# Modulation sums in four pieces between pieces of projections, and layer norms behind the experts by half rows

## What is computed

```python
def first_block(...):                     # one layer
    c_act = jax.nn.silu(c)
    mod = (c_act @ ada_w[i] + ada_b[i])   # 1024 -> 6*1024: six slices
    h = rmsnorm(x, g) * (1.0 + sc1) + sh1
    x = x + g1 * rmsnorm(windowed_gqa_sink(h, ...), ...)
    h = rmsnorm(x, ...) * (1.0 + sc2) + sh2
    x = x + g2 * rmsnorm(swiglu(h, ffn_w_in, ffn_w_out), ...)

def second_block(...):                    # two layers, with modulations of their own
    for i in range(2):
        sh1, sc1, g1, sh2, sc2, g2 = jnp.split(silu_c @ ada_w[i] + ada_b[i], 6, axis=-1)
        yx = mixer_ab(...) if i == 0 else mixer_pool(...)   # differential attention + gate; pooling
        xs = layer_norm(alpha * xs + g1 * yx, ln_g[i, 0], ln_b[i, 0])
        hx = modulate(xs, sh2, sc2)
        fx = peer(hx, peer_wq[i], peer_keys[i], peer_u[i], peer_v[i])   # 128 experts a token, gathered
        xs = layer_norm(alpha * xs + g2 * fx, ln_g[i, 1], ln_b[i, 1])
    return xs

def layer_norm(h, g, b):
    mu = jnp.mean(h, axis=-1, keepdims=True)
    var = jnp.mean(jnp.square(h - mu), axis=-1, keepdims=True)
    return (h - mu) * lax.rsqrt(var + LN_EPS) * g + b
```

## Time and profile before

| | us |
|---|---|
| median of 3 runs | 2122.01 (2121.99 to 2124.06) |
| the profiled execution's own time | 2130.78 |
| its span, first to last instruction | 2128.9 |
| feed-forward input, 22 parts | about 222 to 336 |
| feed-forward output, 11 parts | about 336 to 405 |
| product stage | about 429 to 690 |
| expert stage 0, expert stage 1 | about 725 to 1381, 1480 to 2118 |
| norm and output of token tile 1 | 2117.8 to 2128.9 |

### The profile page before, as it was taken

How to read it: one execution, slowest core, us unless ns; L and a number is a source line. 1 busy time by engine, 2 the same in 40 slices (tenths; PEclk the granted TensorE clock), 3 DMA queues, 4 the chain that set the end, 5 groups by cost and what they waited for, 6 DMA issues and landing times.

```text
span 2128.9 us, 22402 instructions
## 1 busy us (share of the span) xinstructions
PE 1796.7 (84%) x7293; PEld 1085.8 (51%) x7293; DVE 1458.7 (69%) x3023; ACT 911.5 (43%) x2383; POOL 617.7 (29%) x573
## 2 busy tenths in 40 slices
PE   4888999899998899997777787988998877877776
PEld 3757998788887544443222222455654422322222
DVE  6676857677866767766676677527677667677675
ACT  2446433434464344444344444424444444444442
POOL 1160000000000434444334334213444444443441
PEclk9888989899999899999999999999999999999999
DMA  9753758555664899999999999966999999999995
GB/s 368 278 198 119 263 192 298 199 203 213 218 218 144 320 421 421 421 421 420 419 421 422 421 421 421 371 239 273 409 415 421 421 421 421 422 421 421 421 422 242
DMA packets 114693, 723.80 MB, mean 340 GB/s; under 512 B 11504, under 2 KB 13344, under 8 KB 34064
## 3 DMA queue, kind: packets, MB, share of 16 engines
q0 software_dynamic: 74864, 540.30, 61.3%
q1 hardware_dynamic: 39712, 182.07, 23.4%
HBM read 721.24 MB, written 1.08 MB: 339 GB/s over the span
## 4 chain that ended last, share of the span: by engine, by line
DMA 36%; PE 31%; DVE 16%; ACT 7%; issue 5%; POOL 3%; another core or an unknown queue 0%; SPq 0%; DVEq 0%; ACTq 0%; POOLq 0%
DMA X<-in_k_uv,EI 20%; DMA Z<-in_k_uv,EI 12%; PE PS L2183 11%; PE PS L1875 3%; PE PS L1876 3%; PE PS L1877 3%; DVE junk L1862 3%; PE PS L2159 3%; DVE WL L1505 3%; DVE ACC L1489 3%; DMA W<-in_k_uv,EI 2%; POOL X L1047 2%; PE PS L1968 2%; DMA W<-in_ada_w 2%; ACT WH L1056 1%
## 5 line engine op out<-in xcount | busy, mean ns | idle before, releaser
L2183 PE MATMUL PS<-X,dg 128*128 128x512 f32 x1380 | 663.5, 613 | 132.1 <-ACT dg L1056 131.0
L1862 DVE CUSTOM_DVE_ANT_0 junk<-H,X 128x1024 f32<-128x1024 f32 x345 | 421.9, 1223 | 244.5 <-DMA X<-in_k_uv,EI 232.2
L1047 POOL DMA_INDIRECT X<-in_k_uv,EI x345 | 370.1, 1073 | 509.4 <-PE PS L2183 307.8
L2183 PEld LDWEIGHTS PS<-X,dg 128*128 128x128 f32 x1380 | 248.8, 193 | 507.3 <-ACT dg L1056 295.4
L1056 ACT ACTIVATE CF<-DOT 128x1 f32<-128x1 f32 x512 | 103.6, 202 | 666.2 <-DVE DOT L1862 662.6
L2183 PE MATMUL PS<-Z,dg 128*128 128x512 f32 x480 | 237.2, 621 | 65.1 <-ACT dg L1056 64.9
L1056 ACT ACTIVATE dg<-CP,CG 128x128 f32<-128x128 f32 x512 | 205.5, 401 | 17.6 <-PE PS L2183 1.0
L1862 DVE CUSTOM_DVE_ANT_0 junk<-H,Z 128x1024 f32<-128x1024 f32 x120 | 146.8, 1223 | 94.4 <-DMA Z<-in_k_uv,EI 90.9
L2183 PEld LDWEIGHTS PS<-Z,dg 128*128 128x128 f32 x480 | 84.2, 191 | 198.3 <-ACT dg L1056 132.8
L1875 PE MATMUL PS<-XH,WH 128*128 128x256 f32 x592 | 177.0, 299 | 3.6 <-DVE WL L1505 2.1
L1876 PE MATMUL PS<-XL,WH 128*128 128x256 f32 x592 | 172.7, 292 | 0.0
(11 more groups left out here) (314 smaller groups left out, 2599.5 us busy)
## 6 DMA issues: line engine op xcount, KB each, us to landing
W<-in_ada_w SPq DMA_DIRECT2D x56, 1024.0 KB, 5.3
Y<-in_ada_w SPq DMA_DIRECT2D x16, 1024.0 KB, 5.9
W<-in_k_win SPq DMA_DIRECT2D x16, 1024.0 KB, 5.0
W<-in_k_ffi SPq DMA_DIRECT2D x13, 1024.0 KB, 6.0
Y<-in_k_ffi SPq DMA_DIRECT2D x9, 1024.0 KB, 4.9
W<-in_ffn_w_out SPq DMA_DIRECT2D x8, 1024.0 KB, 5.6
W<-in_peer_wq SPq DMA_DIRECT2D x8, 1024.0 KB, 13.0
W<-in_ab_w_out SPq DMA_DIRECT2D x6, 1024.0 KB, 5.2
```

What stands on the lines that cost most here:

```text
L1047: e.indirect_dma_start(out=WS[k][:, :], out_offset=None, in_=I[f"k_uv{ly}"][:, :], in_offset=bass.IndirectOffsetOnAxis(ap=EI[t][:, j:j + 1 ...
L1862: e.tensor_tensor_reduce(junk, H[:, t, :], d[:, 0:D], 1.0, 0.0, ALU.mult, ALU.add, DOT[:, j:j + 1]).then_inc(v_dot, 1)
L2183: p = e.matmul(PS[:, 2 * t + q, :], dgb[n % 4][:, :], d[:, D + q * 512:D + (q + 1) * 512], start=(j == 0), stop=(j == 127))
```

## The change

**Sums in pieces.** A new `gemm_mod(n, s)` places a quarter of part n, then a quarter of sum s (four of its 16 columns), four times over, and `mod` behind. It is used for i = 16 with s = 3, for i = 17 with s = 4, and for i = 7 of the output with s = 5. In the product stage a sum that is due goes out in four pieces, one in each following gap (`sums()`), from the first call of `step` after its eighth slab on; `mod` follows the fourth. `step` may now be called in 14 gaps k = 0 instead of 12. In TensorE's program `modp` takes the bank with its first piece and signals with its last.

**Norms by halves.** `brn` and `frn` multiply, add and take statistics of columns 0 to 511 first, and of columns 512 to 1023 then. The first half waits for a new semaphore `p_lo`, which the first 512-column matmul of a tile's last expert gives. In `frn 1` a new `finish` merges the normalisation with scale and shift: for each half (x - mean) * R5, and then times the reciprocal root plus R1; the first of these passes stands ahead of the wait for ScalarE's root. Step `x, 7` is gone. The output of tile 1 leaves in two DMAs of 256 KB.

```diff
+    def gemm_mod(n, s, *banks):
+
+        for q in range(4):
+            P("gq", n, q, *banks)
+            P("modp", s, 3, q)
+        P("mod", s, 3)
...
-        if i == 16:
-            mod(3, 3)
-            mod(4, 3)
-        gemm(n, bank(low))
+        if i in (16, 17):
+            gemm_mod(n, i - 13, bank(low))
+        else:
+            gemm(n, bank(low))
...
         if i == 7:
-            mod(5, 3)
-        gemm(n)
+            gemm_mod(n, 5)
+        else:
+            gemm(n)
...
-    due = []
+    due, ripe = [], []
 
     def step(b):
 
-        if len(due) > 1:
-            mod(due[0], b)
-            due.clear()
-        elif due:
-            due.append(None)
+        if due:
+            ripe.append(b)
             return
         m = next(steps, None)
         if m is not None:
             ada(m)
             if m in mods:
-                due.append(mods[m])
+                due.extend((mods[m], part) for part in range(4))
+
+    def sums():
+
+        if due and ripe:
+            s, part = due.pop(0)
+            P("modp", s, ripe[0], part)
+            if part == 3:
+                P("mod", s, ripe[0])
+                ripe.clear()
...
-    places = (1, 2, 3, 4, 5, 6, 7, 8, 9, 10, 11, 13)
+    places = range(14)
...
     P("frn", 1)
-    P("x", 7)
     P("out", 1)
...
+            def sum_halves(name, t, y, row, done):
+
+                for half in range(2):
+                    z = slice(512 * half, 512 * half + 512)
+                    w.wait_ge(p_dg if half else p_lo, done if half else done // 128)
+                    q = e.tensor_tensor(H[:, t, z], y[:, z], row[:, z], ALU.mult)
...
+                    e.scalar_tensor_tensor(out=XS[:, t, z], in0=XS[:, t, z], scalar=ALPHA, in1=H[:, t, z],
+                                           op0=ALU.mult, op1=ALU.add).then_inc(v_own, 1)
+                    w.wait_ge(v_own, own.up())
+                    e.bn_stats(bs[:, t, half, :], XS[:, t, z]).then_inc(v_own, 1)
...
+                for half, c in enumerate(halves):
+                    e.scalar_tensor_tensor(out=XS[:, t, c], in0=XS[:, t, c], scalar=mv[:, t, 0:1], in1=R[5][:, c],
+                                           op0=ALU.subtract, op1=ALU.mult).then_inc(v_own, 1)
+                    if half == 0:
+                        w.wait_ge(a_rt, place)
+                        e.reciprocal(z, z).then_inc(v_rs, 1)
+                        w.wait_ge(v_rs, place)
+                    w.wait_ge(v_own, own.up())
+                    e.scalar_tensor_tensor(out=XS[:, t, c], in0=XS[:, t, c], scalar=z, in1=R[1][:, c],
+                                           op0=ALU.mult, op1=ALU.add).then_inc(v_x, 1)
...
+                    lo, hi = (4 * a[2], 4 * a[2] + 4) if len(a) > 2 else (0, 16)
...
-                    for j in range(16):
+                    for j in range(lo, hi):
...
+                        if j == 127 and q == 0:
+                            p.then_inc(p_lo, 1)
```

More of the change, by code:

```diff
@@ L284, in make_plan @@
             step(5)
+        sums()
         next(g)
@@ L981, in _ @@
                     t = a[0]
-                    w.wait_ge(v_x, nth("x", 6 + t))
                     ov = out.rearrange("b (t p) d -> p (b t) d", p=128)
-                    e.dma_start(ov[:, t, :], XS[:, t, :]).then_inc(d_out, 16)
-            w.wait_ge(d_out, 32)
+                    w.wait_ge(v_x, nth("x", 6) + t)
+                    if t:
+                        e.dma_start(ov[:, t, 0:512], XS[:, t, 0:512]).then_inc(d_out, 16)
+                        w.wait_ge(v_x, nth("x", 6) + 2)
+                        e.dma_start(ov[:, t, 512:1024], XS[:, t, 512:1024]).then_inc(d_out, 16)
+                    else:
+                        e.dma_start(ov[:, t, :], XS[:, t, :]).then_inc(d_out, 16)
+            w.wait_ge(d_out, 48)
         @block.gpsimd
@@ L1386, in normalize @@
                 z = mv[:, t, 1:2]
+                e.tensor_scalar(z, z, LN_EPS, None, ALU.add).then_inc(v_ms, 1)
+                return z
+            def normalize(name, t):
+                z = spread_of(t)
                 place = nth.rs[name]
-                e.tensor_scalar(z, z, LN_EPS, None, ALU.add).then_inc(v_ms, 1)
                 w.wait_ge(a_rt, place)
@@ L1392, in normalize, with finish @@
                 e.tensor_scalar(XS[:, t, :], XS[:, t, :], mv[:, t, 0:1], z, ALU.subtract, ALU.mult).then_inc(v_rn, 1)
+            def finish(name, t):
+                z = spread_of(t)
+                place = nth.rs[name]
+                halves = [slice(512 * half, 512 * half + 512) for half in range(2)]
+                w.wait_ge(d_r5, 64)
+                w.wait_ge(d_r1, 64)
+                for half, c in enumerate(halves):
[5 more added lines that the diff above has]
+                        w.wait_ge(v_rs, place)
+                    w.wait_ge(v_own, own.up())
+                    e.scalar_tensor_tensor(out=XS[:, t, c], in0=XS[:, t, c], scalar=z, in1=R[1][:, c],
+                                           op0=ALU.mult, op1=ALU.add).then_inc(v_x, 1)
             def affine(dst, src, grow, brow):
@@ L1965, in _ @@
                     w.wait_ge(v_ada, vada(8 * MOD_SLICE[s] + 7))
-                    take(b)
-                    for j in range(16):
+                    if lo == 0:
+                        take(b)
+                    for j in range(lo, hi):
                         p = e.matmul(PS[:, b, j:j + 1], src[:, j * 128:(j + 1) * 128], ones[:, 0:1],
                                      start=True, stop=True)
-                    p.then_inc(p_mod, 1)
-                    free[b] = [(v_mod, s + 1)]
+                    if hi == 16:
+                        p.then_inc(p_mod, 1)
+                        free[b] = [(v_mod, s + 1)]
                 elif kind == "xp":
```

29 lines of the change are left out of this document (20 added, 9 removed).

## The result

The changed kernel took 2111.62 us (median of five runs, 2110.99 to 2114.28); the kernel before, in five runs, 2124.06 (2121.99 to 2126.79). The ratio is 0.9937 with a 95% interval of 0.9921 to 0.9952, so it is faster by 0.5 to 0.8%. The forecast was 2107.0 with a range of 2102 to 2117: a gain of 15.0 us against 12.4 between the medians, or 13.4 by the ratio.

What follows compares the result with a forecast made beforehand. Ahead of the experts, TensorE paces the first block's feed-forward and parts of the product stage, VectorE with ScalarE the others. 7.1 + 1.35 + 7.5 - 2.45 + 1.45 = 15.0 us off the median 2122.0 gives 2107.0, range 2102 to 2117.

Steps and rivals of the forecast that it cites:

- A: Feed-forward input: sums 3 and 4 in quarters between quarters of parts 26 and 27, 7.1 us gained.
- D: Norms by halves and smaller last DMA: nothing between the layers, 1.45 us gained at the kernel's end.
- B: Part 39: sum 5 in quarters, so eight 512-column passes avoid the lower clock, 1.35 us gained.
- C: Product stage: sums 6, 7 and 8 in quarters, 7.5 us gained together, less 2.45 us for moved slabs.
- Sum 6: Product stage, where TensorE sets the pace: 1.25 us gained from the clock, with its changes between matmuls.
- Sum 7: Product stage, where ScalarE waited for the K part: 2.7 us from the clock plus 0.87, 3.5 gained.
- Sum 8: Product stage: 2.5 us from the clock plus a little of its own last passes, 2.8 gained.
- slab 65: Product stage, VectorE: moved from an idle stretch to ahead of unit 12's maximum, 1.1 us late (0 to 2.35).
- Slab 71: Between the last OB scaling and the turn of XT, on VectorE: 1.35 us lost (0 to 2.35).
- The first: Product stage: VectorE and ScalarE swallow half or more of the sums' gain; total gain 10 us, 2112; chance 0.20.
- a fall whatever the order: All cut sums: pieces bring the clock down as long as whole sums; gain nil, 2122 to 2120; chance 0.10.
- a clock low over all of a part: Parts with pieces: interleaving holds the clock at 0.50 throughout; about 25 us slower, 2147; chance 0.08.

Runs made afterwards that it cites:

- e4_no_c: Changed kernel with the product stage as before: sums 6 to 8 whole, slabs in their old places; 2115.93 us, ratio 0.9956 to the kernel before.
- e6_tail_only: Kernel before with only the new norms and the output in two halves; ratio 0.9986 to the kernel before.
- e1_banks: Kernel before with sum 4 in bank 4 instead of bank 3, so it no longer waits for sum 3's reader; 2125.42 us.
- e2_whole: Changed kernel with sums 3 and 4 whole, one ahead of part 26 and one ahead of part 27; 2114.56 us.
- e5_early: Changed kernel with three slabs of the product stage in other places, none ahead of unit 12's maximum; 2112.08 us, ratio 0.9931 to the kernel before.
- e3_halves: Changed kernel with sums 3 to 8 in two pieces of eight columns instead of four pieces of four; 2120.09 us.

## Why the prediction was right, and where its terms were off

The time, the sign and the range held: 2111.6 in 2102 to 2117, 12.4 to 13.4 us where 15.0 were forecast. Of the four parts A and D came, each 0.4 above its forecast; B is not shown; of C, 5.0 with its slabs, 2.1 to 4.4 came, against the traces with whole sums of e4_no_c and e6_tail_only. Together that is 7.5 + 0 + 2.1 to 4.4 + 1.8, or 11.4 to 13.7 us, and fits the time.

**A, forecast 7.1: 7.5**, in every trace of the code with pieces. The mechanism was right; only the price of changing between matmuls was nearly nothing. The forecast's own sum had slipped there: six changes at 0.08 are 0.48 a part, and it booked 0.24 (part 26 would take 9.74, not 9.5, and A would be 6.6 to 6.7). Both alternatives that would have undone it are out: the clock falls without the idle wait too (e1_banks), and behind a single whole sum (e2_whole).

**B, forecast 1.35: not shown.** The first pair of traces differs by 1.55 in this stage, which looks like a hit, but the second trace of the old code lacks the difference. The step that failed was to take the eight slow passes of the earlier trace rows for a property of the code. The stage took 73.59 with pieces and 73.59 with the whole sum in the second trace of that code. Two kernels with 72.0, one with a whole and one with a cut sum, lack another low stretch of the same stage (328 to 332 in the changed kernel). With a low stretch in one trace of three behind the whole sum, and in none of eight over the pieces, pieces may save half a microsecond there over many runs (an estimate, a third of 1.55); these runs can't tell.

**C, forecast 7.5 for the sums less 2.45 for the slabs: 2.1 to 5.8.** Against the first trace of before the stages 6 to 8 and the turn shrink by 3.5 in the first trace of the changed kernel and by 5.8 in the second; against e4_no_c by 2.1 and 4.3; against e6_tail_only (235.01) by 2.2 and 4.4. Sum 6, forecast 1.25, gave 1.6 or, against the other three traces with whole sums, 3.2. Sum 7, forecast 3.5, gave 1.8 to 4.8. Sum 8, forecast 2.8, reached unit 11's exponentials (2.7 us more lead) and was gone at unit 12. The term mis-sized is slab 65: taken at 1.1 out of 0 to 2.35, it lay there with its whole 2.3 between the weight split and the maximum, and the experiment without it gave back 1.6; the other 0.9 are lost at this place in e5_early too, and what they are stays open. Stage 8 as a whole is no better than before, and 1.5 worse than in e4_no_c. What the clock gave in it and what the new places of the slabs took can be told apart, because the whole sum 8 of e1_banks had no low stretch. The whole stage, in e1_banks (sum whole, slabs in their old places) and in the changed kernel:

```profile
547.26:630.31 83.05, 74.81 (x535) 65.02 (x534) 63.39 (x94) 50.95 (x100) 0.00 (x0) 0.98 0.61 214
540.36:626.21 85.85, 77.07 (x551) 67.42 (x551) 63.48 (x94) 51.15 (x99) 0.00 (x0) 0.98 0.58 209
```

At the same mean clock the changed kernel takes 2.8 us longer (2.7 in its second trace). The trace of before, with the product stage of e1_banks and 6.8 us at the lower clock at sum 8, takes 2.8 more as well; its other low stretch of this stage, at 629 to 637, hardly counts, since e4_no_c with 6.8 us and e6_tail_only with 3.4 us there both take 84.35. So the clock's share of sum 8 was forecast rightly (2.8), and the new order of the stage took all of it back, where 1.1 was booked.

**Slab 71, forecast 1.35 lost: the number was met and the reason was not.** The turn is 1.36 longer in the first trace, 0.8 in the second. But e5_early has the same 1.38 without the slab, and e3_halves has the slab without them. The time was that of passes at the lower clock behind TensorE's idle time of 2.2 us, an idle time that the trace of before and e3_halves have too, with the clock at 1.00 behind it. So this term cost nothing that the runs show. Had only the first trace been read, the wrong cause would have stood as shown.

**D, forecast 1.45: 1.8.** VectorE began 0.75 before the last matmul's end (0.86 forecast). The fused add took 0.69 with a fixed factor, where I had taken the 0.75 of an operation with a factor per row. From the first operation to the statistics it is 4.23 (forecast 4.34). From there to the last DMA 3.4 us, against 3.6 forecast (whose terms add up to 3.76) and 4.2 before. The last DMA took 2.5 until the end of the span against 3.1 with twice the bytes: 0.6, where I had taken 0.5. No run takes the halves, the merged passes and the two DMAs apart; this split is read from the timelines alone.

**The rivals.** The first, that VectorE and ScalarE swallow part of C, is what happened at sum 8, by a slab that the change itself had put there; the 10 us that it gave in all are 2.4 to 3.4 less than were measured, the forecast's 15.0 are 1.6 to 2.6 more. The runs lie between the two. That the measured 2111.6 falls on this rival's 2112 is an accident of the base (below). Pieces among small matmuls and transposes did keep the clock up: 1.00 at sums 6 and 8 in both traces, and at sum 7 in one of them. The rule that spoke against it (the Trainium skill, TensorE: Matmul & The Clock Gate, Part 4: PE-mode transpose) did not decide here. The other two, a fall whatever the order and a clock low over all of a part, are refuted by the same rows and by those of parts 26 and 27.

**The base.** The forecast took the gain from a median of three runs, 2122.0. With more runs the kernel before is at 2124 to 2126, so the same gain would have given 2109 to 2111. And the profiled executions differ by 19.2 where the kernels differ by 13: 3.1 us of it lie in the expert stages and ahead of the feed-forward input, where nothing was changed but the norm between the layers, 1.0 between the turn and the first expert, and more in low stretches that the first trace of before happened to have.

## What to carry to other kernels

Cut a long row of tiny matmuls and put the pieces between dense ones: with pieces of four columns the granted clock stayed up at all but one of 37 sums here, with pieces of eight at all but two of six, and a piece costs no more than its share. A gap of an engine was free here only behind the last operation that another engine waited for; look at what the first small operation behind the gap starts, and place the moved work behind it. Before a stage's gain is put down to an edit, take a second trace of the same code, since low stretches of the clock wander and each is worth about 1.5 us here. Charge what the change moves to the stage where it lands: here it took back all that the clock had given at sum 8.

## What the runs showed of the hardware that I had not expected

The same code has its low stretches of the clock in different places from run to run: behind a whole sum of 32 one-column passes the clock stayed at 1.00 in two traces of three at sum 5 and fell in all of them at the pair. A row of such passes keeps TensorE's records at 100% busy, and the clock falls on it all the same. Sixteen one-column passes at a time, with 24 passes of 256 columns between them, left it at 1.00 over 17.6 us; sixteen behind 1 us of idle time, in the product stage, did not (0.51 over the 6 us that follow). And the output DMA of half the size, 256 KB instead of 512, was only 0.6 us shorter from its issue to the end of the span, 2.5 against 3.1: by these two sizes most of its time does not go with the bytes. A fused add with a fixed factor took 0.69 us on 512 columns, with a factor per row 0.75.
